# Down products of a mixture-of-experts block by row group over four PSUM banks, with the output copies in one burst

## The reference

```python
expert = g_idx * EXPERTS_PER_GROUP + e_idx
gate = jnp.sum(jax.nn.one_hot(expert, N_EXPERTS, dtype=F32) * weights[..., None], axis=1)
h = jax.nn.silu(jnp.einsum('td,edf->tef', xf, w_gate)) * jnp.einsum('td,edf->tef', xf, w_up)
y = jnp.einsum('tef,te,efd->td', h, gate.astype(h.dtype), w_down)
```

## Time and profile before

| | |
|---|---|
| runs | 1498.04, 1500.74, 1501.60 us |
| span of the profiled execution | 1495.6 us |
| PE busy | 1436.0 us (96%) |
| DVE busy | 1013.3 us (68%) |
| ACT busy | 773.7 us (52%) |
| POOL busy | 195.5 us (13%) |
| read from and written to HBM | 313.56 and 40.73 MB |

### The profile page before, as it was taken

How to read it: one execution, slowest core, us unless ns; L and a number is a source line. 1 busy time by engine, 2 the same in 40 slices (tenths; PEclk the granted TensorE clock), 3 DMA queues, 4 the chain that set the end, 5 groups by cost and what they waited for, 6 DMA issues and landing times.

```text
span 1495.6 us, 24307 instructions
## 1 busy us (share of the span) xinstructions
PE 1436.0 (96%) x9391; PEld 1288.1 (86%) x9391; DVE 1013.3 (68%) x1283; ACT 773.7 (52%) x912; POOL 195.5 (13%) x99
## 2 busy tenths in 40 slices
PE   8999999999999999999996899999999999999995
PEld 7999999999999999999996458888888888888782
DVE  4247746747767787423025668889888888888787
ACT  4245445444444433311110057788778777777774
POOL 0000000000000000234330001221211212222130
PEclk9999999999999999999998899999999999999998
DMA  7321231322213312633435599999999999999997
GB/s 273 111 89 57 96 103 61 113 72 85 92 59 111 113 57 74 203 127 140 152 102 204 192 387 379 384 393 387 392 381 375 388 387 392 387 384 384 359 294 232
DMA packets 89749, 335.36 MB, mean 224 GB/s; under 512 B 12086, under 2 KB 18790, under 8 KB 60874
## 3 DMA queue, kind: packets, MB, share of 16 engines
q1 hardware_dynamic: 84202, 315.54, 56.5%
q0 software_dynamic: 5472, 18.74, 5.0%
HBM read 313.56 MB, written 40.73 MB: 237 GB/s over the span
## 4 chain that ended last, share of the span: by engine, by line
PE 79%; DVE 10%; DMA 5%; ACT 4%; issue 2%; ACTq 0%; SPq 0%; DVEq 0%; POOL 0%; POOLq 0%
PE BANK L1780 12%; PE BANK L1781 12%; PE BANK L1782 12%; PE BANK L2143 6%; PE BANK L2145 6%; PE BANK L2144 6%; PE BANK L2192 4%; DMA RAWB<-in_w_up 4%; PE BANK L2190 4%; PE BANK L2191 4%; PE BANK L2127 2%; DVE LOB L1647 2%; PE BANK L1922 1%; PE BANK L1798 1%; ACT SC L878 1%
## 5 line engine op out<-in xcount | busy, mean ns | idle before, releaser
L1780 PE MATMUL BANK<-XH,HI 128*128 128x260 f32 x1746 | 502.8, 288 | 1.5 <-DVE RT L1462 1.0
L1647 DVE TENSOR_TENSOR LOB<-RAWB,HIB 128x2048 fp32r<-128x2048 f32 x196 | 448.5, 2292 | 72.4 <-ACT HIB L1035 71.9
L1781 PE MATMUL BANK<-XL,HI 128*128 128x260 f32 x1746 | 495.5, 284 | 0.0
L1782 PE MATMUL BANK<-XH,LO 128*128 128x260 f32 x1746 | 494.7, 283 | 0.0
L1035 ACT ACTIVATE HIB<-RAWB 128x2048 fp32r<-128x2048 f32 x196 | 376.2, 1920 | 97.0 <-PE BANK L2145 65.1
L1780 PEld LDWEIGHTS BANK<-XH,HI 128*128 128x128 f32 x1746 | 331.1, 190 | 2.8 <-issue 1.9
L1781 PEld LDWEIGHTS BANK<-XL,HI 128*128 128x128 f32 x1746 | 331.1, 190 | 0.7
L1782 PEld LDWEIGHTS BANK<-XH,LO 128*128 128x128 f32 x1746 | 331.2, 190 | 0.0
L2143 PE MATMUL BANK<-HIB,XGH 128*128 128x512 f32 x512 | 201.4, 393 | 6.6 <-issue 3.0
L2145 PE MATMUL BANK<-LOB,XGH 128*128 128x512 f32 x512 | 199.5, 390 | 0.0
L2144 PE MATMUL BANK<-HIB,XGL 128*128 128x512 f32 x512 | 199.3, 389 | 0.0
(11 more groups left out here) (371 smaller groups left out, 1637.9 us busy)
## 6 DMA issues: line engine op xcount, KB each, us to landing
RAWB<-in_w_down SPq DMA_DIRECT2D x68, 1024.0 KB, 11.1
RAWB<-in_w_gate SPq DMA_DIRECT2D x67, 1024.0 KB, 10.6
RAWB<-in_w_up SPq DMA_DIRECT2D x67, 1024.0 KB, 10.8
RAW<-in_w_in SPq DMA_DIRECT2D x39, 1024.0 KB, 5.0
RAW<-in_w_out SPq DMA_DIRECT2D x16, 1024.0 KB, 5.6
Y<-in_xT SPq DMA_DIRECT2D x8, 520.0 KB, 8.9
RT<-in_xT SPq DMA_DIRECT2D x16, 260.0 KB, 5.3
x_rows<-R SPq DMA_DIRECT2D x5, 832.0 KB
```

The costliest lines, as they stand in the source:

```text
L1647: dve.tensor_tensor(LOB[:, s, :], RAWB[:, r, :], HIB[:, s, :].bitcast(F32), ALU.subtract).then_inc(b_lo[s], 1)
L1780: pe.matmul(bank, hw[:, c, :], h, start=(c == 0), stop=False)
L1781: pe.matmul(bank, hw[:, c, :], l, start=False, stop=False)
L1782: ins = pe.matmul(bank, lw[:, c, :], h, start=False, stop=(c == KC - 1))
```

## The change

It has five parts.

1. A down tile holds one row group c (128 of the 512 rows) with all 2048 columns. In DRAM its 2048 numbers of a partition are one row of 8 KB, where the tile of before had four pieces of 2 KB.
2. `down` multiplies such a tile into four banks, 512 columns each, three matmuls per bank. The banks are complete only after the fourth tile. They are banks 2, 4, 5 and 7, and 0, 1, 3 and 6 for block nb.
3. ACT copies the four banks in one burst (`out_copies`), after the last tile. In the loop it stands at the end of an iteration; `down` waits, at its first tile, for all four copies of the block before.
4. The turned tokens use banks 6 and 3 instead of 2 and 3 (`t_bank`). Bank 6 is also that of the turned h, so `tokens` and `turn_h` have one more wait each.
5. After the loop the copies of block `last` stand in one burst ahead of the splits of tiles 2 and 3 of block nb, and the copies of block nb in one burst behind them and behind the small square root that loads ACT's table.

```diff
--- before.py
+++ after.py
@@ -464,6 +464,14 @@
 
             return ((0, 1, 2, 3), (6, 7, 4, 5))[k % 2][n]
 
+        DOWN_BANK, LAST_DOWN_BANK = (2, 4, 5, 7), (0, 1, 3, 6)
+
+        def t_bank(g, j):
+
+            if g % 2:
+                return 3
+            return 2 if isinstance(j, int) and j == 0 else 6
+
         def first_tile(i):
 
             return RAWB[:, i, :] if i < NRAW else RAW67[i - NRAW][:, :]
@@ -661,12 +669,12 @@
             def down(j, first):
                 e = sp.value_load(EBI[0:1, bass.ds(j - 1, 1)], min_val=0, max_val=NE - 1)
                 for n in range(4):
-                    w = a["w_down"][bass.ds(e, 1), :, :, 512 * n:512 * n + 512].rearrange("a p c n -> p (a c) n")
+                    w = a["w_down"][bass.ds(e, 1), :, n, :].rearrange("a p n -> p (a n)")
                     i = first + n
                     s = i % NRAW
                     sp.wait_ge(b_lo[(2 + i) % NHL], (2 + i) // NHL + 1 + 4 * (j - 1))
                     passed(sp)
-                    sp.dma_start(RAWB[:, s, :].rearrange("p (c n) -> p c n", c=4), w).then_inc(b_raw[s], 16)
+                    sp.dma_start(RAWB[:, s, :], w).then_inc(b_raw[s], 16)
 
             gate_up(1, 0)
             down(1, 8)
@@ -1050,16 +1058,17 @@
             def token_hi(g, j):
 
                 act.wait_ge(b_tx, 4 * j + g + 1)
-                act.activation(XGH[:, 4 * g:4 * g + 4, :], BANK[:, 2 + g % 2, :].rearrange("p (c n) -> p c n", c=4), ACT.Copy).then_inc(b_xh, 1)
+                act.activation(XGH[:, 4 * g:4 * g + 4, :], BANK[:, t_bank(g, j), :].rearrange("p (c n) -> p c n", c=4), ACT.Copy).then_inc(b_xh, 1)
 
             def h_hi(j, into=HTH):
                 act.wait_ge(b_th, j + 1)
                 act.activation(into[:, :, :], BANK[:, 6, :].rearrange("p (c n) -> p c n", c=4), ACT.Copy).then_inc(b_hh, 1)
 
-            def out_copy(n, i, j, into=YO):
+            def out_copies(j, i=11, into=YO, banks=DOWN_BANK):
 
                 act.wait_ge(b_used, 12 * j - 3 + i)
-                act.activation(into[:, 512 * n:512 * n + 512], BANK[:, 4 + n % 2, :], ACT.Copy).then_inc(b_y, 1)
+                for n in range(4):
+                    act.activation(into[:, 512 * n:512 * n + 512], BANK[:, banks[n], :], ACT.Copy).then_inc(b_y, 1)
 
             act.sem_inc(b_y, 2)
             for g in range(4):
@@ -1080,38 +1089,29 @@
                     silu(j)
                     token_hi(0, j + 1)
                     bhi(10, 0, j)
-                    act.wait_ge(b_yw, 16 * j)
-                    out_copy(0, 8, j)
                     token_hi(1, j + 1)
                     bhi(11, 0, j)
-                    out_copy(1, 9, j)
                     token_hi(2, j + 1)
                     bhi(0, 0, j + 1)
-                    out_copy(2, 10, j)
                     token_hi(3, j + 1)
                     bhi(1, 0, j + 1)
-                    out_copy(3, 11, j)
+                    act.wait_ge(b_yw, 16 * j)
+                    out_copies(j)
             h_hi(last - 1)
             for i in range(2, 10):
                 bhi(i, 0, last)
             silu(last)
             bhi(10, 0, last)
-            act.wait_ge(b_yw, 16 * last)
-            out_copy(0, 8, last)
             bhi(11, 0, last)
-            out_copy(1, 9, last)
             h_hi(last, HTH2)
             bhi(0, 0, nb)
-            out_copy(2, 10, last)
             bhi(1, 0, nb)
-            out_copy(3, 11, last)
-            bhi(2, 0, nb)
-            out_copy(0, 0, nb, YO2)
-            bhi(3, 0, nb)
-            for n in range(1, 3):
-                out_copy(n, n, nb, YO2)
+            act.wait_ge(b_yw, 16 * last)
+            out_copies(last)
+            for i in range(2, 4):
+                bhi(i, 0, nb)
             act.activation(MV2[:, 0, 3:4], EPS_LN2, ACT.Sqrt)
-            out_copy(3, 3, nb, YO2)
+            out_copies(nb, 3, YO2, LAST_DOWN_BANK)
 
 
             def samples_copy(n):
@@ -1654,7 +1654,7 @@
 
             def token_lo(g, j):
                 dve.wait_ge(b_xh, 4 * j + g + 1)
-                dve.tensor_tensor(XGL[:, 4 * g:4 * g + 4, :], BANK[:, 2 + g % 2, :].rearrange("p (c n) -> p c n", c=4),
+                dve.tensor_tensor(XGL[:, 4 * g:4 * g + 4, :], BANK[:, t_bank(g, j), :].rearrange("p (c n) -> p c n", c=4),
                                   XGH[:, 4 * g:4 * g + 4, :].bitcast(F32), ALU.subtract).then_inc(b_xl, 1)
 
             def h_lo(j, into=HTL, high=HTH):
@@ -2121,10 +2121,11 @@
                     pe.wait_ge(s_x1, 4 * NT + 4 + g + 1)
                 elif g == 0:
                     pe.wait_ge(b_xg, 16 * j)
+                    pe.wait_ge(b_hl, j - 1)
                 if not isinstance(j, int) or j >= 1:
                     pe.wait_ge(b_xl, 4 * j + g - 1)
                 for c in range(4):
-                    ins = pe.transpose(BANK[:, 2 + g % 2, 128 * c:128 * c + 128], XG[:, 4 * g + c:D:KC], IDENT[:, :])
+                    ins = pe.transpose(BANK[:, t_bank(g, j), 128 * c:128 * c + 128], XG[:, 4 * g + c:D:KC], IDENT[:, :])
                 ins.then_inc(b_tx, 1)
 
             def ready(i, m0, j):
@@ -2171,25 +2172,27 @@
                     if i in (1, 2):
                         tokens(i + 1, 0)
 
-            def turn_h(j):
+            def turn_h(j, after=None):
                 pe.wait_ge(b_h, j + 1)
                 if not isinstance(j, int):
                     pe.wait_ge(b_hl, j)
+                if after is not None:
+                    pe.wait_ge(b_xl, after)
                 for c in range(4):
                     ins = pe.transpose(BANK[:, 6, 128 * c:128 * c + 128], H[:, c:512:4], IDENT[:, :])
                 ins.then_inc(b_th, 1)
 
-            def down(n, i, j, th=HTH, tl=HTL):
-
-                if n == 0:
+            def down(c, i, j, th=HTH, tl=HTL, banks=DOWN_BANK):
+
+                if c == 0:
                     pe.wait_ge(b_hl, j)
-                pe.wait_ge(b_y, 4 * (j - 1) + n + 1)
+                    pe.wait_ge(b_y, 4 * (j - 1) + 2)
                 hw, lw = ready(i, 0, j)
-                b = BANK[:, 4 + n % 2, :]
-                for c in range(4):
-                    pe.matmul(b, th[:, c, :], hw[:, c, :], start=(c == 0), stop=False)
-                    pe.matmul(b, tl[:, c, :], hw[:, c, :], start=False, stop=False)
-                    ins = pe.matmul(b, th[:, c, :], lw[:, c, :], start=False, stop=(c == 3))
+                for n in range(4):
+                    b = BANK[:, banks[n], :]
+                    pe.matmul(b, th[:, c, :], hw[:, n, :], start=(c == 0), stop=False)
+                    pe.matmul(b, tl[:, c, :], hw[:, n, :], start=False, stop=False)
+                    ins = pe.matmul(b, th[:, c, :], lw[:, n, :], start=False, stop=(c == 3))
                 ins.then_inc(b_used, 1)
 
             for g in range(2):
@@ -2197,21 +2200,21 @@
             first_gate_up()
             for g in range(4):
                 tokens(g, 1)
-            turn_h(0)
+            turn_h(0, 7)
             with pe.Fori(1, MAXB) as j:
                 with pe.If(j < last):
                     gate_up(j, 0)
                     for n in range(4):
                         tokens(n, j + 1)
                         down(n, 8 + n, j)
-                    turn_h(j)
+                    turn_h(j, 4 * j + 7)
             gate_up(last, 0)
             for n in range(4):
                 down(n, 8 + n, last)
                 if n == 1:
                     turn_h(last)
             for n in range(4):
-                down(n, n, nb, HTH2, HTL2)
+                down(n, n, nb, HTH2, HTL2, LAST_DOWN_BANK)
 
             pe.wait_ge(f_add, 1)
             for n in range(4):
```

## The result

| | before | changed |
|---|---|---|
| median of the runs, us | 1500.89 (1498.04 to 1501.6, 4 runs) | 1515.13 (1515.0 to 1517.06, 4 runs) |
| ratio to before | | 1.0107, 95% interval 1.0091 to 1.0124 |
| span of the profiled execution, us | 1495.6 | 1513.2 |

The changed kernel is 1.1% slower, 14 to 16 us; 1518.0 was forecast, in a range of 1504 to 1530.

What follows compares the result with a forecast made beforehand. The loop was taken as bound by PE, with transfers almost late. Terms 13.6 + 0.2 - 2.6 + 6.1 = +17.3 us on a 1495.6 us span gave 1512.9; with 5.1 around the span, 1518 us, range 1504 to 1530.

Steps and rivals of the forecast that it cites:

- The burst in the loop: At 14 loop block boundaries, three more copies delay tile 2's split, so PE waits 0.97 us each: +13.6 us.
- The transfers: Longer w_down rows save DMA time; as PE bounds the blocks, only the loop's late landings go: -2.6 us.
- The down products and banks: Down matmuls in another order, changing bank every third matmul, cost nothing extra: 0.
- The exit: Behind the fifteenth block, the three copies fit under ACT's idle 4.27 us leaving the loop: +0.2 us, bounds 0 to 1.5.
- The new waits of PE: Token transposes, turn_h and down gain waits on low halves or copies, all satisfied in time: 0.
- The end: After the last blocks, four queued scatters delay the load of X and DVE's first addition: +6.1 us, bounds +3.5 to +10.5.
- PE's delay: At the end, PE's last products wait for four copies (+2.3), its YO2 sum for one (+0.85): +3.2, beside the 6.1.
- What lies around the span: The median of the runs lies 5.1 us above the profiled span, a distance kept for the changed kernel.
- The burst was not hidden: Rival: the loop's copy burst is hidden and only the end counts, 1504 us; chance 0.08.
- the transfers don't set the pace: Rival: transfers set block length, so longer rows gain 12.2 us over 17 blocks, 1494.6 us; chance 0.05.
- a change of bank costs nothing: Rival: each change of bank in the down products costs 0.09 us, 24.5 us in all, 1543 us; chance 0.05.
- the clock did not fall: Rival: PE loses its full clock in the down matmuls of 17 blocks, near 1689 us; chance 0.02.

Runs made afterwards that it cites:

- experiment 2: Changed kernel with the copy of h and the split of tile 2 ahead of the loop's burst of four output copies: 1511.56 us.
- experiment 7: Changed kernel with output copies spread behind the splits of tiles 2 to 5 of the next block, and POOL's gather issued ahead of the scatter: 1502.01 us.
- experiment 5: Kernel before with only the down tiles read as 8 KB rows, not 2 KB pieces (wrong weights, so only its time counts): 1496.29 us.
- experiment 6: Changed kernel with each row of a down tile moved in four 2 KB pieces (wrong weights, time unaffected): 1517.03 us.
- the two experiments with the column order: Kernel before with 8 KB rows: 1496.29 us; changed kernel with copies spread, gather ahead, old token banks, last two blocks by columns: 1497.74 us.
- the first four experiments: Changed kernel with copies spread, burst behind tile 2's split, no copy wait for block nb, or block 1's tokens in old banks: 1609.48, 1511.56, 1513.56, 1516.26 us.
- experiment 1: Changed kernel with the loop's four output copies spread, one behind each split of tiles 2 to 5 of the next block: 1609.48 us.
- experiment 3: Changed kernel, but block nb's down products no longer wait for the four copies of block last: 1513.56 us.

## Why the prediction was right, step by step

*The burst in the loop* (+0.97 a block, 13.6 in all) was right in its mechanism, its place and almost its size. The chain and the 14 waits show it, T+7.17 stands where 1.47 less the slack of 0.5 had put it, and experiments 2 and 7 move the cost and remove it. The term came out at 1.12 a block, 15.75 over blocks without a late landing: what it lacked is the 0.15 by which a tile behind a wait is longer. The slow first matmul makes up most of it; the earlier trace rows show one like it behind transposes (0.32 for 0.23), which I used only for a rival.

*The transfers* (-2.6): right to the tenth in the traces, 13.19 = 15.75 - 2.56 us for the loop (the medians of experiment 5 say 2.4 to 5.9). Experiments 5 and 6 show that the cause I gave first, fewer and longer packets, was enough but not needed.

*The down products and banks* (0): right. Matmuls in the new lines stand 0.23 us apart over each change of bank (1061.24, 1061.47, 1061.69), and with the copies out of the way the blocks are exactly as long as before.

*The exit* (+0.2): the copies did fit under the gap. The +0.8 measured goes with the low clock behind PE's gap, where I had relied on its staying at 1.00 (before, PE waited once more for a low half there, which the slower matmuls hid). Experiment 5 has the same 0.8 without any copy burst, so it needs no part of the burst.

*The new waits of PE* (0): turn_h of block 0 waited 0.9 us for the low half of the tokens, which is not made in any shadow, since there are no down products in front of it. But before, PE waited 1.0 us for the same half right behind turn_h, so the wait itself cost nothing. The 0.9 us up to the first loop block go for the most part with the low clock behind the wait's new place (39.02 us from the last token transposes to turn_h of block 1, before 38.24); for that the prediction had no term.

*The end* (+6.1, bounds 3.5 to 10.5) was the wrong size, +2.7 between the two traces and under its lower bound, and it hung on the wrong path. The step that failed is "Everything up to the end follows from these additions". The end follows from PE's sum over YO2: the chain runs through it in both kernels, and in the trace of experiment 5 DVE began 1.4 us earlier than in that of before (T+13.7, not T+15.1) and the chain passed to it at the same T+25.34. The prediction had PE's delay, +3.2, and set it aside as "less than 6.1 and beside it"; it came out at +3.5, of which the waits for copies are 2.2 and 0.7.

The 6.1 of the load's path was wrong too. The four scatters did take POOL's time as supposed (the last is issued 6.5 us after the first; three times 2.05 is 6.15), but "with 8.4 us for it until SP's load" read the time from the last scatter's issue to SP's load as a fixed price. It was 4.9 in the changed kernel (1471.33 to 1476.27), and 6.6 and 7.8 in the two experiments with the column order, so that DVE began at T+18.2 and not at T+21.2. In the trace of before the last scatter ran beside transfers that filled the DMA engines (share 1.04 from 1452 to 1456 us), in the changed kernel beside few (0.37 from 1471 to 1476). That this is the reason was argued and not tried. With the load at T+21.2 its path would have been the longer of the two, since DVE had only some 0.5 us to spare.

*What lies around the span* (5.1) failed too. In every run it was 1.8 to 1.9 us (1515.0 with a span of 1513.2). The profiled execution of before, with 1495.6, was a short one: the spans of before's nine runs beside the first four experiments lie between 1494.9 and 1500.0. Some of the difference may be late landings, of which that trace had few: experiment 5 took away 4.1 us by the medians, 2.6 by this trace. No trace of a longer execution of before is at hand to show it.

So the time was close because two errors, 3.4 us too much at the end and 3.2 around the span, met 3.7 too little: 2.1 in the slow first matmuls, 0.9 up to the first block, 0.6 at the exit. 1518.0 - 6.6 + 3.7 = 1515.1. The mechanism of the loop, 13.2 of the 17.6 us, was right; that the other errors left only 2.9 us between forecast and measurement was luck.

*The rivals.* The burst was not hidden; the transfers don't set the pace (experiment 5: no block under 35.15); a change of bank costs nothing; the clock did not fall in the loop between its second and its fifteenth block.

## What to carry to other kernels

An output copy that moves from beside the products to behind the last of them costs nothing by itself; it costs what stands behind it in its engine's queue, less the slack there. Work that slack out from one boundary of the trace (end of the last product, start of the first matmul that needs the split), and put the copies one by one between the splits, where each has a tile's slack. Before an operation is made later, look also at the queue of the engine that waits for it: the same spreading cost 94 us while a gather stood behind the scatter, and gained 13 once they had changed places. And a wait between two events seen once is not the price of the second: ask which other release could have come last, and follow the chain of before to its last piece. Here it ran through PE's sum, and not through the load that I forecast.

## What the runs showed of the hardware that I had not expected

*The same short gap lowered the clock in one execution and not in another.* The kernel before and experiment 5 issue the same instructions at the loop's exit, and PE stands idle there for 3.0 us in both. Windows of the two, before first, columns as above:

```profile
1416.00:1420.00 4.00, 3.91 (x18) 2.91 (x16) 2.60 (x2) 3.91 (x4) 0.07 (x1) 1.00 0.64 197
```

```profile
1412.00:1416.00 4.00, 4.00 (x11) 3.16 (x12) 0.98 (x2) 2.40 (x2) 0.00 (x0) 0.59 0.90 281
```

One stayed at 2.4 GHz, the other ran matmuls at 0.43 us instead of 0.23 for some 3 us; the stretch between turn_h of block 15 and that of block "last" was 31.74 and 32.57 us. Behind this gap the clock fell in eight of the ten traces and stayed at 1.00 in those of before and of experiment 1. At the start of the loop the changed kernel fell to 0.57 in a window of 4 us behind a wait of 0.9 us, and experiment 3, with the same instructions up to there, kept 1.00. A gap of 0.8 us in each of the 14 blocks of the changed kernel's loop never lowered the clock; those of 5 to 7 us in experiment 1 did at each of the four that I read by windows.

*POOL issues indirect scatters that wait for nothing 1.9 to 2.7 us apart* (1464.84, 1466.75, 1468.63, 1471.33). From the first issue to the last they need 6.5 us, where scatters that follow their copies need 8.6 (1441.24 to 1449.86); but a burst of copies ahead of them delays the first, from T-6.8 to T+1.9.

*A gather took 9.4 to 12.5 us to land beside the stream of weights* (experiment 1, DMA share 1.02), more than the 5.5 to 7.2 us by the medians of a 1 MB weight tile in the same kernel.
